# A block on one core: another order of loads, scores and modulations in the first part

## The reference

```python
mod = c @ ada_w + ada_b                       # 6 x 1024 numbers from one row c
sh1, sc1, gt1, sh2, sc2, gt2 = split(mod, 6)
h = rmsnorm(x, norm1_g) * (1.0 + sc1) + sh1
xr, yr, q, k, v, ga, gb = split(h @ w_in)     # each 8 heads of 128 columns
y_a = rg_lru(conv(xr)) * gelu(yr)             # per head: two gates, a recurrence in time
q, k = head_rmsnorm(q), head_rmsnorm(k)
y_b = stick_breaking_attention(q, k, v)       # softplus of the scores, sums from the right, exp
x = x + gt1 * ((sigmoid(ga) * y_a + sigmoid(gb) * y_b) @ w_out)
```

## Time and profile before

| what | value |
| --- | --- |
| median of three runs | 1683.41 us |
| time of the profiled execution | 1686.51 us |
| its span | 1684.5 us |
| mean granted TensorE clock | 0.988 |
| TensorE busy | 1634.4 us |
| VectorE busy | 1000.5 us |
| ScalarE busy | 806.0 us |
| GpSimd busy | 810.6 us |

### The profile page before, as it was taken

The page is one execution under the profiler, slowest core; times in us unless marked ns, Lnnn a source line. Parts: engine busy times, 40 slices in busy tenths (PEclk is TensorE's granted clock), DMA queues, the critical chain, the costliest instruction groups (busy, mean ns, idle before and its releaser), DMA issues.

```text
span 1684.5 us, 19467 instructions
## 1 busy us (share of the span) xinstructions
PE 1634.4 (97%) x7178; PEld 1323.1 (79%) x7178; DVE 1000.5 (59%) x1212; ACT 806.0 (48%) x1011; POOL 810.6 (48%) x583
## 2 busy tenths in 40 slices
PE   6699999999999999999999999999999999999997
PEld 3567877777778888888888888888888888888885
DVE  6468988888647718616633767566337554155541
ACT  4356666666544425423443333677554444244442
POOL 2234454544555455445566454455574353453525
PEclk9899999999999999999999999999999999999999
DMA  8423323443323232332323232212222121321212
GB/s 321 176 89 121 114 93 135 138 138 100 99 82 112 88 100 94 95 131 94 100 88 98 84 106 61 72 44 64 67 88 88 58 92 51 109 91 62 89 51 75
DMA packets 46605, 166.80 MB, mean 99 GB/s; under 512 B 5168, under 2 KB 5296, under 8 KB 46000
## 3 DMA queue, kind: packets, MB, share of 16 engines
q1 hardware_dynamic: 46512, 165.57, 30.1%
HBM read 163.45 MB, written 2.10 MB: 98 GB/s over the span
## 4 chain that ended last, share of the span: by engine, by line
PE 93%; DVE 3%; ACT 2%; issue 1%; DMA 1%; POOL 0%; POOLq 0%; SPq 0%; ACTq 0%; DVEq 0%
PE lin L685 17%; PE lin L686 17%; PE lin L687 17%; PE big L685 7%; PE big L686 7%; PE big L687 7%; PE big L813 1%; PE m_bo L831 1%; PE m_bo L703 1%; PE m_bo L701 1%; PE m_bo L702 1%; PE big L1116 1%; PE big L1118 1%; PE big L1117 1%; PE big L824 1%
## 5 line engine op out<-in xcount | busy, mean ns | idle before, releaser
L651 POOL TENSOR_TENSOR w_lo<-raw,w_hi 128x512 fp32r<-128x512 f32 x198 | 287.8, 1453 | 622.8 <-ACT w_hi L1155 622.6
L685 PE MATMUL lin<-h_hi,w_hi 128*128 128x512 f32 x912 | 360.6, 395 | 0.0
L686 PE MATMUL lin<-h_lo,w_hi 128*128 128x512 f32 x912 | 355.9, 390 | 0.0
L687 PE MATMUL lin<-h_hi,w_lo 128*128 128x512 f32 x912 | 355.6, 390 | 0.0
L654 POOL TENSOR_TENSOR w_lo<-raw,w_hi 128x512 fp32r<-128x512 f32 x207 | 307.5, 1486 | 13.9 <-ACT w_hi L1155 13.9
L1155 ACT ACTIVATE w_hi<-raw 128x1024 fp32r<-128x1024 f32 (+1 forms) x207 | 215.4, 1041 | 200.3 <-DMA raw<-weights 49.7
L686 PEld LDWEIGHTS lin<-h_lo,w_hi 128*128 128x128 f32 x912 | 171.7, 188 | 37.0 <-issue 1.9
L685 PEld LDWEIGHTS lin<-h_hi,w_hi 128*128 128x128 f32 x912 | 171.5, 188 | 37.2 <-issue 1.9
L687 PEld LDWEIGHTS lin<-h_hi,w_lo 128*128 128x128 f32 x912 | 171.6, 188 | 36.2
L651 POOL TENSOR_TENSOR qk_hl<-raw,qk_hl 128x512 fp32r<-128x512 f32 x43 | 59.8, 1390 | 126.3 <-ACT qk_hl L1155 126.3
L685 PE MATMUL lin<-y_hi,w_hi 128*128 128x512 f32 x260 | 102.2, 393 | 1.7 <-issue 1.7
(11 more groups left out here) (511 smaller groups left out, 3444.0 us busy)
## 6 DMA issues: line engine op xcount, KB each, us to landing
raw<-weights SPq DMA_DIRECT2D x245, 512.0 KB, 3.5
slab<-ada SPq DMA_DIRECT2D x32, 512.0 KB, 4.4
scr<-ada SPq DMA_DIRECT2D x16, 512.0 KB, 6.7
raw<-weights SPq DMA_DIRECT2D x10, 256.0 KB, 2.6
x<-x_t SPq DMA_DIRECT2D x2, 1024.0 KB, 8.5
out_t<-scr SPq DMA_DIRECT2D x8, 256.0 KB, 2.6
raw<-weights SPq DMA_DIRECT2D x4, 448.0 KB, 3.4
rgw<-rg_w SPq DMA_DIRECT2D x1, 1024.0 KB, 7.3
```

The costliest lines, as they stand in the source:

```text
L651: nc.gpsimd.tensor_tensor(lo[:, 0:4 * P], raw[:, s, 0:4 * P], hi[:, 0:4 * P].bitcast(F32), ALU.subtract).then_inc(w_half, 1)
L685: nc.tensor.matmul(psum_of(n), wh, hi(k), start=(k == 0), stop=False)
L686: nc.tensor.matmul(psum_of(n), wh, lo(k), start=False, stop=False)
L687: last = nc.tensor.matmul(psum_of(n), wl, hi(k), start=False, stop=(k == nk - 1))
```

## The change

- **Ring.** xr 0 comes ahead of slabs 16 to 18; yr 0 and ga 0 follow; slabs 19, 20 and 21 stand around gb 0. Loop 1 of ring_plan adds nothing. In loop 2 slabs 22 and 23 stand between k and the slab ahead of v. From loop 3 on the ring is as it was. The first three slabs of the ring no longer wait for modulation 16; slab j still waits for modulation j - 3.
- **Modulations.** Head 0 runs 16 after k's norm. Head 1 runs 17 and 18 ahead of shares, 19 to 21 after k's norm, 22 after mix. Head h > 1 runs 4h - 1, 4h and 4h + 1 (counted from 16) after k's norm and 4h + 2 after mix; before it was 4h, 4h + 1, 4h + 2 and 4h + 3.
- **Start.** c comes from the host spread over 128 partitions and is loaded (c_rows) between the halves of x; the spread and the two matmuls are gone, and ScalarE copies it to PSUM after its second square. Slabs wait for the first half of x and weights follow slabs 1, 3, 5, 7, 11. keep_clock adds two half-width matmuls ahead and three full ones in steps 1 and 2.
- **Lanes.** q 1 comes two chunks a step from step 4, k 1 wholly in step 7; the splits of q 1 and k 1 stand at k = 4 and 6.
- **Scores of head 0** come after v 1, its head square and xr 0 instead of after v 1. Low squares of k come ahead of shares for h < 2.
- **Banks** of the two-bank ring start with the other one.
- **h_low** is waited for by a number that is written out.

```diff
@@ ring_plan
-            units += [("ada", a + i, 8) for i in range(3)] + [("xr", 0, 8)] + [("ada", a + i, 8) for i in (3, 4)]
+            units += [("xr", 0, 8)] + [("ada", a + i, 8) for i in range(3)] + [("yr", 0, 8), ("ga", 0, 8)]
+            units += [("ada", a + 3, 8), ("gb", 0, 8), ("ada", a + 4, 8), ("ada", a + 5, 8)]
             continue
-        if 1 < h < HEADS:
-            units += [("q", h, 8), ("k", h, 8), ("ada", a, 8), ("v", h, 8)]
+        if h == 1:
+            continue
+        if h < HEADS:
+            units += [("q", h, 8), ("k", h, 8)] + [("ada", a - 2 + i, 8) for i in range(2 if h == 2 else 0)]
+            units += [("ada", a, 8), ("v", h, 8)]
@@ LANES, bank_plan
-         (("v", 0), (0, 0, 3, 4, 5, 6, 7, 8)), (("q", 1), (0, 0, 0, 0, 3, 6, 7, 8)),
-         (("k", 1), (0, 0, 0, 0, 0, 0, 3, 8)))
+         (("v", 0), (0, 0, 3, 4, 5, 6, 7, 8)), (("q", 1), (0, 0, 0, 0, 2, 4, 6, 8)),
+         (("k", 1), (0, 0, 0, 0, 0, 0, 0, 8)))
+SPLIT_AT = (0, 1, 2, 4, 6)
-    bank, before, last, turn = {}, {}, {}, {2: 0, 5: 0}
+    bank, before, last, turn = {}, {}, {}, {2: 1, 5: 0}
@@ sync
+            sp.dma_start(c_row, c_rows).then_inc(c_loaded, 16)
             sp.dma_start(x[:, 4:8], x_t[:, 4:8]).then_inc(x_loaded[1], 16)
+            sp.wait_ge(x_loaded[0], 16)
             for i in range(ADA_FIRST):
-                if i in (0, 2, 4, 9, 12):
-                    load_weights((0, 2, 4, 9, 12).index(i))
...
+                if i in (1, 3, 5, 7, 11):
+                    load_weights((1, 3, 5, 7, 11).index(i))
...
-                    sp.wait_ge(ada_used, max(j - NA + 1, ADA_FIRST))
+                    if r >= NA:
+                        sp.wait_ge(ada_used, j - NA + 1)
@@ tensor
+            pe.wait_ge(par_loaded, 16)
+            keep_clock(2, lin[:, 0, 0:T // 2], par[:, 0:P], par[:, 0:T // 2])
             pe.wait_ge(cst_loaded, 16)
-            pe.wait_ge(c_spread, 1)
-            for i in range(2):
-                last = nc.tensor.matmul(m_bo[:, i], c_("ones"), c_row[:, i * T:(i + 1) * T], start=True, stop=True)
-            last.then_inc(c_turned, 1)
...
+                if step in (1, 2):
+                    keep_clock(3 - step, big[:, 2], c_("ones"), x[:, 0])
...
                 if g == 0:
                     unit("v", h, H, L)
+                    head_square(3)
+                    unit("xr", 0, H, L)
...
-                if h < HEADS:
+                if h != 1:
                     if g > 0:
                         pe.wait_ge(gate_r_read, g)
                     head_square(2 * h + 1)
-                if g >= 0:
+                if g > 0:
                     unit("xr", g, H, L)
@@ scalar
-                if k == 3:
-                    act.wait_ge(c_turned, 1)
-                    nc.scalar.activation(c_row, c_row_ps, ACT.Copy).then_inc(c_copied, 1)
+                if k == 1:
+                    act.wait_ge(c_loaded, 16)
+                    nc.scalar.activation(c_row_ps, c_row, ACT.Copy).then_inc(c_copied, 1)
@@ vector
                 square_low(2 * h + 1)
+                if h < 2:
+                    square_low(2 * h + 2)
+                if h == 1:
+                    modulate(ADA_FIRST + 1)
+                    modulate(ADA_FIRST + 2)
                 if g >= 0:
                     shares(g)
                     sum_later(0)
-                square_low(2 * h + 2)
+                if h > 1:
+                    square_low(2 * h + 2)
...
-                else:
-                    modulate(ADA_FIRST)
...
-                if g >= 0:
+                if h == 0:
+                    modulate(ADA_FIRST)
+                elif h == 1:
+                    modulate(ADA_FIRST + 3)
+                    modulate(ADA_FIRST + 4)
+                    modulate(ADA_FIRST + 5)
+                else:
+                    modulate(ADA_FIRST + 4 * h - 1)
                     modulate(ADA_FIRST + 4 * h)
-                modulate(ADA_FIRST + 4 * h + 1)
-                modulate(ADA_FIRST + 4 * h + 2)
-                if h == 0:
-                    modulate(ADA_FIRST + 3)
+                    modulate(ADA_FIRST + 4 * h + 1)
...
                     mix(g)
-                    if h < HEADS - 1:
-                        modulate(ADA_FIRST + 4 * h + 3)
+                    modulate(ADA_FIRST + 4 * h + 2)
```

More of the change, by code:

```diff
@@ L209, with build @@
 OUT_UNITS = (("w_out", 0), ("ff_down", 16), ("a_out", 0), ("r_out", 8))
-def build(nc, ada, weights, params, consts, rg_w, x_t, positions, inv_counts, out_t):
+def build(nc, ada, weights, c_rows, params, consts, rg_w, x_t, positions, inv_counts, out_t):
     ctx = ExitStack()
@@ L245, in build @@
         ada_used = sem("ada_used")
-        c_spread = sem("c_spread")
-        c_turned = sem("c_turned")
+        c_loaded = sem("c_loaded")
         c_copied = sem("c_copied")
@@ L577, in _ @@
                 sp.dma_start(ada_in[:, i % 6], ada[:, i]).then_inc(ada_loaded[i % 6], 16)
+                if i in (1, 3, 5, 7, 11):
+                    load_weights((1, 3, 5, 7, 11).index(i))
             for g, (kind, j, nk) in enumerate(RING):
-                if (kind, j) == ("xr", 0):
+                if (kind, j) == ("gb", 0):
                     sp.dma_start(rgw[:], rg_w).then_inc(rgw_loaded, 16)
@@ L792, in chunk @@
                     last.then_inc(unit_done, 1)
+            pe.wait_ge(par_loaded, 16)
+            keep_clock(2, lin[:, 0, 0:T // 2], par[:, 0:P], par[:, 0:T // 2])
             pe.wait_ge(cst_loaded, 16)
-            pe.wait_ge(c_spread, 1)
-            for i in range(2):
-                last = nc.tensor.matmul(m_bo[:, i], c_("ones"), c_row[:, i * T:(i + 1) * T], start=True, stop=True)
-            last.then_inc(c_turned, 1)
             for k in range(DK):
                 square(k + 1, k == 0, k == DK - 1)
-            keep_clock(3, lin[:, 0], c_("ones"), x[:, 0])
+            keep_clock(3, big[:, 2], c_("ones"), x[:, 0])
             for step in range(DK):
+                if step in (1, 2):
+                    keep_clock(3 - step, big[:, 2], c_("ones"), x[:, 0])
                 pe.wait_ge(h_low, step + 1)
@@ L1261, in _ @@
             for k in range(DK):
-                if k in (0, 1, 2):
-                    split_ahead(0, k)
-                if k in (4, 5):
-                    split_ahead(0, k - 1)
+                if k in SPLIT_AT:
+                    split_ahead(0, SPLIT_AT.index(k))
                 high(0, k)
@@ L1679, in _ @@
             dve.wait_ge(cst_loaded, 16)
-            v.tensor_tensor(c_row.rearrange("p (k t) -> p k t", t=P),
-                            c_("ident").unsqueeze(1).broadcast_to([P, DK, P]),
-                            pall("c").unsqueeze(2).broadcast_to([P, DK, P]), M).then_inc(c_spread, 1)
-            dve.wait_ge(c_spread, 1)
             v.tensor_copy(ones_r[:], c_("ones")).then_inc(dve_order, 1)
@@ L1698, in norm_apply @@
                                                in1=h_hi[:, e].bitcast(F32), op0=AD, op1=SU).then_inc(h_low, 1)
-                        dve.wait_ge(h_low, counted(h_low))
+                        dve.wait_ge(h_low, DK * r + e + 1)
             def gain_low(gain, k):
@@ L1758, in _ @@
                                            in1=h_hi[:, e].bitcast(F32), op0=AD, op1=SU).then_inc(h_low, 1)
-                    dve.wait_ge(h_low, counted(h_low))
+                    dve.wait_ge(h_low, e + 1)
             z = big_f[:, 0:1280]
@@ L2425 @@
         "weights": weights,
+        "c_rows": np.ascontiguousarray(np.broadcast_to(i["c"].reshape(1, D), (P, D))),
         "params": np.ascontiguousarray(params),
```

## The result

The changed kernel takes **1724.65 us** (median of four runs, 1722.51 to 1725.85) beside 1683.39 for the kernel before on the same chip: ratio 1.0241, 95% interval 1.0223 to 1.0259, so 41 us slower. The forecast was 1713.0 with a range up to 1725. The profiled execution after took 1722.51 us with a span of 1720.6. It is the fastest of its four, while the profiled one of before was 3.1 us above its median. That is why the spans lie 36.1 us apart and the medians 41.3.

What follows compares the result with a forecast made beforehand. TensorE, busy 97% of the span, was taken to bound the kernel. Six heads' cost of 39.6 us less 7.5 at the start and 2.5 in the tail gave +29.6, so 1713.0 us against the 1683.4 median; range 1698 to 1725.

Steps and rivals of the forecast that it cites:

- The late weight: Heads 1 to 6: gb's weight, queued behind a slab awaiting a later pass, makes TensorE wait 4.9 us, up to 5.8.
- The rule on the ports: First pass after k's norm: GpSimd and VectorE share SBUF interfaces, so without a split it takes 1.28 us, not 2.20.
- The six heads: Heads 1 to 6: wait 4.9 us plus clock loss 1.7 each, cost 39.6 us, bounds 28 and 46.
- the clock term: Behind each wait at gb, TensorE runs at a low clock: loss 1.7 us a head, 1.9 as upper end.
- yr's weight, late behind slab a+1: Steady heads: yr's weight lands later, ScalarE blocks 3.9 us, but hidden from TensorE with 0.6 us to spare at worst.
- The start: Up to ga of head 0: earlier chunks and no long wait for yr's weight, gain 7.5 us, bounds 5 and 9.7.
- The tail: End of the block: w_out 0 takes a long-free bank, no wait or clock loss; gain 2.5 us, bounds 0 and 3.5.
- The sum: Whole kernel: 39.6 - 7.5 - 2.5 = +29.6 us, 1713.0 against the median.
- (a): Rival at gb in the steady heads: the late weight is hidden, only the gains stay, 1673 us; chance 0.12.
- (b): Rival in the heads: yr's weight misses its 0.6 us too, 1 to 3 us more a head, say 1724; chance 0.12.
- (c): Rival at gb in six heads: the wait without the clock loss, +19.4 us, 1703; chance 0.08.

## Why the prediction was right, step by step

**The late weight: right, and nearly to the number.** Named were the first pass after k's norm, a chain of 8.8 us from its end to the split weight, and a wait of 4.9. Measured are 149.84 to 158.74, 8.9 us, and waits of 4.76 in head 1 and 4.7 in the mean (28.3 / 6). The pass took 1.28 us, the end that I took, not 2.20: GpSimd has no row between the end of the split before and 156.25. The rule on the ports in the Trainium skill ("GPSIMD Engine Reference", Specifications) had pointed to the same end. But I read the 1.28 from a wrong row. The pass at 135.53 does have company; GpSimd's timeline before shows it:

```profile
135.66 2.31 POOL L651 TENSOR_TENSOR w_lo<-raw,w_hi 128x512 fp32r<-128x512 f32 x1 [3.63 <-ACT w_hi L1155]
```

That pass was short because it had started 0.13 us ahead of GpSimd, which took 2.31 us instead of 1.29; the pass at 155.03 started 0.63 us behind it. The pass at 159.51 (1.28 us, GpSimd idle) is the row that supports the number. The number was right, its reading in part luck.

**The six heads: the term was 39.6 and is 45.2**, or 7.54 us a head instead of 6.6. Of these 4.7 are the wait and 0.5 the new wait before weights_turned (4.6 us less head 0's 1.8, over six). The remaining 2.3 are clock, where I took 1.7 and 1.9 at most. My 1.7 came from a gap of 3.6 us at another place, and the 4.2 us behind the wait in head 1 show the same (4.21 x 0.40 = 1.7). But in heads 3 to 6 the same 4.2 us are wholly at 1.2 GHz (granted 0.50) and these heads lose 2.5 to 2.6. So the clock term was right in kind and 0.6 us a head too small, 3.8 us in all: the largest part of what this term missed.

**The missed half microsecond.** The prediction followed yr's weight, late behind slab a+1, to TensorE and found it hidden. It is: TensorE starts yr without waiting. But ScalarE stands still for it (4.63 us, 135.46; I had written 3.9), and behind ScalarE's split in its own queue wait the copy of v and the root of q's norm. VectorE waits 1.95 us for that root (138.66), the exponents come later, and TensorE waits 0.4 to 0.7 before weights_turned. I had asked who waits for the weight, not who waits for the engine that waits for the weight. With gb's weight already ahead of its slab, putting yr's ahead of slab a+1 took the period from 49.3 to 48.1.

**The start: gain 7.5 forecast, 7.2 in the profile.** Four of the other kernels have the same instructions up to the gate matmuls of head 0 and stand there at 111.83 to 113.09, so this execution (111.65) was a good one and against the one profile of before the gain is 5.8 to 7.2. The steps hold: scores ended at 82.9 (81.5 to 83.3), chunks ended at 65.0 (64.3), no wait of 10 us on ScalarE. What I didn't see is that a better start was to be had: the loader's order alone gives 10.3. I costed the later scores only by what they cover, not by what they hold up.

**The tail: gain 2.5 forecast, 1.8 measured.** w_out no longer waits, and products 7 wait 1.5 us for turned_weights, the item that I had set against it. The clock loss of 1.8 that I added to the bank's 1.7 is not reliable, as the old turn of the banks showed.

**The sum.** -7.2 + 45.2 - 1.8 = +36.2, the difference of the spans (36.1). The forecast sum was +29.6; 5.6 of the missing 6.6 are the six heads. The medians stand 41.3 apart, 5.2 more than the spans, only because of which executions were profiled: that of before was 3.1 above its median, that of after 2.1 below. My range had no term for this, though the three runs of before already spread by 2 us. The profiled execution after also had the higher granted clock, 0.985 against 0.981 and 0.982 in its three others, so in those the clock may have cost still more; they have no profile that would show it. The measured median lies 0.35 us inside the upper edge and the highest run outside it: the mechanism was right, that the range still held the time was partly luck.

**The rivals.** That the late weight is hidden (a) is refuted by the six waits. The worse chain (b) has its time, 1724, but not its mechanism: yr was not late for TensorE. ScalarE waited for it, and that makes 2.8 of the 5.6 us; the clock makes 3.8, and the waits for gb's weight came out 1.1 below the forecast. The wait without the clock loss (c) is refuted by the granted clock of 0.60 and by the matmuls that removed it.

## What to carry to other kernels

When a pass that frees a slot is moved later, write down everything that stands behind that slot's load in the same issue queue, and then everything that stands behind the engine which waits for each of these: here gb's weight, a wait of 4.7 us a head; yr's, 0.5 us a head, and 1.2 once gb's is mended; and, by the rows, the next head's q, 1.2 us a head that shows only when the other two are mended. Putting the weights ahead of the slabs in the queue removes most of it without touching the compute. And where a chain of other engines hangs on one piece of TensorE's work, as the softplus on the scores, fill TensorE's hole with work behind that piece rather than in front of it: that was worth 6 us at the gate matmuls of head 0.

## What the hardware showed that I had not expected

- Gaps of 1.73 and 1.74 us ahead of the same matmul of w_out: in two executions the granted clock behind it was 0.55 and 0.52, in two others 1.00. Behind gaps of 4.5 to 4.9 us in the changed kernel it fell each time, and the loss was 1.9 to 2.6 us by head.
- Matmuls that nobody reads, 19 in a gap of 4.8 us, paid for themselves: 8.4 us over six heads by the profiles, though one of the six came out longer. In a single gap of 4.1 us, 15 of them raised the granted clock from 0.50 to 1.00 and shortened their stretch by 1.55 us, while the whole kernel's time did not fall.
- When a pass of VectorE and a half split of GpSimd overlap, the one that starts second takes longer. In the kernel before, from 68 us on, seven passes that started up to 0.26 us ahead of a half took 1.28 to 1.34 us, as they do alone, and the half took 2.18 to 2.37 instead of 1.29; the fourteen that started while a half was under way took 2.19 or 2.20.
- GpSimd's and VectorE's busy time fell by 9 and 15 us in the slower kernel. The work is the same; the two engines met less often (1.27 us for a half split instead of 1.75 and 2.27, 1.28 for a pass instead of 2.20). A page that shows lighter engines is no sign of a faster kernel.
